# Prompt attention of a hybrid decoder layer: rounded high and low score operands, values as stationary half columns, output projection after the attention

## The chip, the cores and the metric

One core of one Trainium2 chip. The metric is the device time of one execution in microseconds (us). Before the change the kernel took 1881.82, 1887.27 and 1888.38 us in three runs, so the median is 1887.27 us. The profile is of another execution of the same program, which took 1884.58 us.

## The reference

One layer in float32 over a prompt of 1024 tokens and 8 sample sequences of one token each, width 1024. What matters here, shortened:

```python
z = rmsnorm(x, norm1_g) @ w_in                      # u, v, q, three pairs of k and v, gates
o_a = gmlp_mix(u, v, ...)                           # 512 columns
s = einsum('bqgrd,bngd->bgrqn', q, k_c) * scale     # 8 heads of 64, 2 key groups
p_c = masked_softmax(s - slopes * dist, dist >= 0)  # compressed branch, 63 keys
imp = einsum('bgqn,nj->bgqj', sum(p_c, axis=2), overlap)
_, idx = lax.top_k(imp, 8)                          # selected branch: 8 of 16 blocks of 64
o_s = softmax over the selected blocks @ v_s
o_w = softmax over the last 512 keys @ v_w          # window branch
o_b = gate0 * o_c + gate1 * o_s + gate2 * o_w
x = x + concat(rmsnorm(o_a), rmsnorm(o_b)) @ w_out
h = rmsnorm(x, norm2_g)
y = rmsnorm(x + (silu(h @ w_gate) * (h @ w_up)) @ w_down, final_norm_g)   # inner width 2816
```

The sample sequences go through the same weights, with keys from a paged cache. The new rows of keys and values are outputs too.

## The kernel before, in words

The five engines have one program each, written out by hand and tied by semaphores. There are five stages, and each engine goes through them in order.

**Stage 1** (lines 298 to 690) normalizes nine row tiles (eight of 128 prompt rows, one of the 8 sample rows), turns them, and multiplies them with w_in in five column chunks (`project`, line 324; the matmul is line 338). A matmul's stationary operand is the turned rows, so the sample tile has 8 stationary columns and still streams all columns of the chunk. `turn_k` (L351) turns the keys into `kT`: 64 rows of key, and 33 rows from a constant that carry position and block (`kaug`), 97 in all. At the end POOL loads a first part of the compressed cache (`load_raw`, L752), behind the store at L555.

**Stage 2** (L719 to 898) builds compressed keys and values; its last group is the prompt. **Stage 3** (L998 to 1259) is the samples' attention. There PE multiplies four sequences in four 32-column strips of its array, with `tile_position` (L1121, L1124, L1129).

**Stage 4** is the prompt's attention in eight query blocks i of 128 rows. One list `events` fixes the order on every engine. A block has 17 units: window heads 0 to 7 (up to 5 key tiles), the compressed branch, selected heads 0 to 7 (i+1 key tiles). For a head, in this order:
- `QK` (L1421): scores of one head, 128 queries by up to 1024 keys, a plain float32 matmul with 97 rows contracted; mask tiles are added by a bf16 matmul (L1426). It writes one of two bank pairs, which it shares with `QT`, `CS`, `SELT`, `OBT`, `WO` and `H2T`.
- DVE takes the row maximum (L1669), ACT the exponential and the row sum (L1552), into one of two buffers.
- `T` (L1490; L1488 for the compressed branch): PE turns each 128 by 128 piece of the probabilities; DVE (L1533) and ACT (L1537) copy the turned pieces out.
- `PV` (L1511, L1507): the turned probabilities are stationary (128 columns), the values of one head stream (64 columns): one matmul for each head and key tile.

At a branch's end `add_branch` (L1634 to L1645) scales and adds. Between the heads stand fillers: `QT` (L1398, copy L1657) turns the queries of the next block, `CS`, `CN`, `CI` (L1404 to L1408, L1595 to L1621) are the compressed softmax and the choice of blocks, `SELT` (L1432, L1676) brings that choice into the query rows. Also between the heads of block i stands the whole tail of tile i-1: `OBQ`, `OBN`, `OBT` (norm and turn of the result, L1443), `WO` (output projection, 16 float32 matmuls of 512 columns, L1452, added by L1696), `H2N` (L1701) and `H2T` (turn, L1470, split into high and low parts by L1573 and L1707).

**Stage 5** is the feed-forward part in 22 steps of 128 inner columns. All operands are split into a rounded high part (type fp32r) and a low part, and each product is three fp32r matmuls: gate and up at L1793 to L1795 (344 columns each), down at L1820 to L1822 (512 columns each). Down runs over nine row tiles and two halves, 18 units a step, each added to `x_all` by DVE (L1923). At the end each tile is normalized (L1934) and stored (L1773).

## Time and profile before

| what | value |
|---|---|
| profiled execution, device time | 1884.58 us |
| its span, first to last instruction | 1882.6 us |
| median of the runs | 1887.27 us |
| PE busy | 1776.3 us, 94% |
| DVE, ACT, POOL busy | 728.5, 390.3, 273.5 us |
| mean granted clock of PE | 0.96 |
| stage 4, first query turn to first gate matmul | 538 to 1083 us |

PE is TensorE's matmul side and PEld its weight loads. Busy time of a group is the time that the union of its records covers; records of PE overlap, since each lasts until its results are out. So how often a matmul can start is read from start times in the timeline, or from a long run of one form. A plain float32 matmul has two records, a transpose and an fp32r matmul have one.

### The profile page before, as it was taken

What the parts mean: (1) busy time and instruction counts of PE and PEld (TensorE: products, weight loads), DVE (VectorE), ACT (ScalarE), POOL (GpSimd) and SP (SyncE); (2) the same over time, 40 slices, a digit from 0 to 9 for tenths busy, and PEclk for the clock granted to TensorE, in tenths of its full rate; (3) what the DMA queues carried; (4) which work ended last, traced back from release to release, by engine and by line L of the source; (5) the groups of instructions that cost most, each with busy time, mean ns of one, the idle gap of its engine ahead of it and who ended that gap; (6) DMA issues with size and microseconds to landing.
All of it is one profiled execution on the core that took longest, in us unless ns stands there. A gap on an engine that the chain in (4) does not pass through costs nothing.

```text
span 1882.6 us, 25099 instructions
## 1 busy us (share of the span) xinstructions
PE 1776.3 (94%) x9317; PEld 1356.1 (72%) x9317; DVE 728.5 (39%) x1319; ACT 390.3 (21%) x862; POOL 273.5 (15%) x286
## 2 busy tenths in 40 slices
PE   7999999698778899999999899999999999999996
PEld 4464454587346666687776698998998998998894
DVE  2100334222224444574565215335335334334437
ACT  2100111122112323332332222112112112112112
POOL 2210121211300000000000113113113112112112
PEclk9999999698967999999999999999999999999999
DMA  8220100533630000000000121211211211211202
GB/s 294 78 89 0 45 1 6 141 90 109 188 107 4 4 4 1 4 4 1 4 1 1 34 68 34 68 33 33 67 33 33 67 33 33 67 33 33 67 11 90
DMA packets 91320, 94.73 MB, mean 50 GB/s; under 512 B 6353, under 2 KB 74546, under 8 KB 91154
## 3 DMA queue, kind: packets, MB, share of 16 engines
q1 hardware_dynamic: 69410, 73.99, 12.8%
q0 software_dynamic: 4240, 11.32, 2.0%
q10 hardware_dynamic: 17600, 8.47, 1.7%
q8 instruction: 46, 0.75, 0.2%
q14 instruction: 24, 0.19, 0.0%
HBM read 86.61 MB, written 11.34 MB: 52 GB/s over the span
## 4 chain that ended last, share of the span: by engine, by line
PE 86%; DVE 5%; issue 3%; DMA 2%; ACT 1%; SPq 1%; ACTq 1%; POOL 0%; POOLq 0%; DVEq 0%
PE bankpair L338 14%; PE bankpair L1793 9%; PE bankpair L1795 9%; PE bankpair L1794 9%; PE bankpair L1452 7%; PE bankpair L1421 6%; PE bankpair L1820 5%; PE bankpair L1511 5%; PE bankpair L1821 5%; PE bankpair L1822 5%; PE bankpair L819 3%; PE bankpair L1490 2%; DMA work<-in_state_win_kv 1%; PE bankpair L1408 1%; PE bankpair L803 1%
## 5 line engine op out<-in xcount | busy, mean ns | idle before, releaser
L1793 PE MATMUL bankpair<-h2T_high,w_high 128*128 128x344 f32 x1056 | 337.9, 320 | 0.0
L1795 PE MATMUL bankpair<-h2T_high,w_low 128*128 128x344 f32 x1056 | 337.1, 319 | 0.0
L1794 PE MATMUL bankpair<-h2T_low,w_high 128*128 128x344 f32 x1056 | 337.1, 319 | 0.0
L338 PE MATMUL bankpair<-work 128*128 128x512 f32 (+3 forms) x720 | 288.2, 557 | 0.8 <-DMA work<-in_w_in 0.8
L1923 DVE TENSOR_TENSOR x_all<-x_all,bankpair 128x512 f32<-128x512 f32 (+1 forms) x396 | 251.7, 684 | 1.7
L338 PEld LDWEIGHTS bankpair<-work 128*128 128x128 f32 (+1 forms) x720 | 127.2, 180 | 145.5 <-issue 136.6
L1909 DVE TENSOR_TENSOR kT_space<-kT_space,bankpair 128x344 f32<-128x344 f32 x66 | 33.9, 513 | 451.4 <-ACT kT_space L1857 451.4
L1793 PEld LDWEIGHTS bankpair<-h2T_high,w_high 128*128 128x128 f32 x1056 | 198.6, 188 | 3.1 <-issue 0.2
L1794 PEld LDWEIGHTS bankpair<-h2T_low,w_high 128*128 128x128 f32 x1056 | 198.1, 188 | 1.1 <-issue 0.2
L1795 PEld LDWEIGHTS bankpair<-h2T_high,w_low 128*128 128x128 f32 x1056 | 198.4, 188 | 0.0
L1844 POOL TENSOR_TENSOR w_low<-work,w_high 128x1024 fp32r<-128x1024 f32 x44 | 105.5, 2421 | 565.5 <-ACT w_high L1839 565.5
L1820 PE MATMUL bankpair<-w_high,act_high 128*128 128x512 f32 (+1 forms) x396 | 158.6, 401 | 3.5 <-DVE x_all L1923 3.5
L1421 PE MATMUL bankpair<-kT_space,work 97*128 97x512 f32 (+3 forms) x384 | 152.6, 503 | 9.8 <-ACT work L1552 3.7
L1857 ACT ACTIVATE kT_space<-bankpair 128x344 f32<-128x344 f32 x66 | 30.3, 459 | 624.3 <-PE bankpair L1795 624.3
L1821 PE MATMUL bankpair<-w_low,act_high 128*128 128x512 f32 (+1 forms) x396 | 157.3, 397 | 0.0
L1822 PE MATMUL bankpair<-w_high,act_low 128*128 128x512 f32 (+1 forms) x396 | 156.0, 394 | 0.0
L1552 ACT ACTIVATE work<-bankpair,small 128x640 f32<-128x640 f32 (+7 forms) x128 | 89.4, 699 | 188.4 <-DVE small L1669 183.4
L1669 DVE TENSOR_REDUCE small<-bankpair 128x1 f32<-128x640 f32 (+7 forms) x128 | 89.9, 704 | 67.4 <-PE bankpair L1426 67.0
L205 POOL TENSOR_SCALAR small<-small 128x1 f32<-128x1 f32 (+1 forms) x45 | 12.6, 280 | 610.1 <-ACT work L1562 371.9
L1421 PEld LDWEIGHTS bankpair<-kT_space,work 97*128 97x128 f32 x384 | 64.9, 202 | 45.0 <-issue 33.3
L1820 PEld LDWEIGHTS bankpair<-w_high,act_high 128*128 128x128 f32 (+1 forms) x396 | 70.0, 177 | 33.8 <-DVE x_all L1923 14.7
L1822 PEld LDWEIGHTS bankpair<-w_high,act_low 128*128 128x128 f32 (+1 forms) x396 | 70.1, 177 | 21.7
(270 smaller groups left out, 2064.3 us busy)
## 6 DMA issues: line engine op xcount, KB each, us to landing
work<-in_w_gate SPq DMA_DIRECT2D x22, 512.0 KB, 5.0
work<-in_w_up SPq DMA_DIRECT2D x22, 512.0 KB, 6.2
work<-in_w_down SPq DMA_DIRECT2D x22, 512.0 KB, 3.8
work<-in_w_in SPq DMA_DIRECT2D x4, 2048.0 KB, 7.9
x_all<-in_x_prompt SPq DMA_DIRECT2D x8, 512.0 KB, 12.2
work<-in_cache_kv_cmp SPq DMA_DIRECT2D x32, 128.0 KB, 2.8
work<-in_cache_kv_cmp POOLq DMA_DIRECT2D x32, 128.0 KB, 2.9
work<-in_cache_kv_slc POOLq DMA_DIRECT2D x32, 128.0 KB, 3.7
```

Of the source, the lines that this page charges most:

```text
L338: ins = pe.matmul(pb(at_n % 4)[0:n, 0:w], hT[:, k, P * t:P * t + n], wslot[c % 2][:, k, 0:w], start=(k == 0), stop=(k == KD - 1))
L1421: ins = pe.matmul(s_pair(e)[:, P * c:P * (c + len(part))], q, kT[0:KAUG, 2 * (kind == "w") + g, P * part[0]:P * part[-1] + P], start=True, ...
L1452: ins = pe.matmul(s_pair(e)[0:n, 512 * half:512 * half + 512], lhs, wo[:, k, 512 * half:512 * half + 512], start=(k == 0), stop=(k == KD - 1))
L1511: ins = pe.matmul(bank_o[:, DH * h:DH * h + DH], pT_buf[n % 4][:, col:col + P], v_all[:, tiles[b], int(kind == "w"), DH * g:DH * g + DH], ...
L1793: pe.matmul(out, wh, high, start=(k == 0), stop=False)
L1794: pe.matmul(out, wh, low, start=False, stop=False)
L1795: ins = pe.matmul(out, wl, high, start=False, stop=(k == KD - 1))
L1820: pe.matmul(out, ah, wh, start=True, stop=False)
L1821: pe.matmul(out, ah, wl, start=False, stop=False)
L1822: pe.matmul(out, al, wh, start=False, stop=True).then_inc(y_ready, 1)
L1844: pool.tensor_tensor(w_low[s][x], w_raw[s][x], w_high[s][x].bitcast(F32), ALU.subtract).then_inc(gu_low, 1)
L1923: dve.tensor_tensor(x, x, bank[2 + (s + t) % 2][0:n, 512 * half:512 * half + 512], ALU.add).then_inc(y_added, 1)
```

## The change

- **Scores.** The queries are rounded (`qT_split`, the same rounded part in both halves of the partitions), and their remainder goes into `qT_aug` with the 33 position rows. The keys are split likewise: `kT_split` holds the rounded part in rows 0 to 63 and the remainder in rows 64 to 127, `kT_aug` the rounded part and the 33 rows. QK and CS become two fp32r matmuls each, with 128 and 97 rows. For this each key or query is turned twice by plain matmuls with the identity, one into each column half of the array.
- **Values.** `T` and `PV` go by key tile ("item") and no longer by head: `T` turns the pieces of 4 heads for each of two key groups; `PV` has the values of a group as stationary operand (64 columns, one column half for each group) and streams 4 heads' probabilities, 512 columns. So all heads' probabilities of a branch are kept (`p_win`, `p_slc`), and the items of one branch stand between the score heads of the next. The result comes out turned: ACT copies it (`OC`), PE turns it back (`ON`), then DVE scales and adds.
- **Output projection.** All `WO`, `H2N`, `H2T` come after the last attention block. `x_all` holds the split operands meanwhile, so the prompt's x is loaded again. The position rows of the queries are loaded by POOL's queue.
- **Sample rows.** In `project`, `WO` and down the 8 sample rows go through the array in four strips, each with a quarter of the columns; down for them is plain float32, one unit for each step in place of two. The sample tile comes first in the last additions.

```diff
@@ project
+                for b in range(NQ):
+                    rows_b, cols_b = strip(b), slice(w // NQ * b, w // NQ * (b + 1))
+                    ins = pe.matmul(pb(at_n % 4)[rows_b, 0:w // NQ], hT[:, k, SEQ:TOK], wslot[c % 2][:, k, cols_b],
+                                    start=(k == 0), stop=(k == KD - 1))
@@ turn_k
-                ins = pe.transpose(pb(6 + m % 2)[0:DH, P * g:P * g + P], kvst[:, m % 2, col + DH * g:col + DH * g + DH],
-                                   ident[:, :])
+                for b in range(2):
+                    ins = pe.matmul(pb(6 + m % 2)[DH * b:DH * b + DH, P * g:P * g + P],
+                                    kvst[:, m % 2, col + DH * g:col + DH * g + DH], ident[:, :], start=True, stop=True,
+                                    tile_position=(0, DH * b), skip_group_check=True)
@@ take_kT
+            link(dve.tensor_copy(split, src))
+            dve.tensor_copy(kT_aug[0:DH, 2 * c:2 * c + 2, P * t:P * t + P], split[0:DH])
+            dve.tensor_tensor(split[DH:P], src[DH:P], split[DH:P].bitcast(F32), ALU.subtract).then_inc(kT_ready, 1)
@@ the order of stage 4
+    def half(i, kind, done, between):
+        heads = [unit_at[i, kind, h] for h in range(NH)]
+        parts = [n for b in done for n in branch_items(b)]
+        for k in range(max(NH, len(parts))):
+            if k < NH:
+                events.append(("QK", heads[k]))
+            if k == 0 and heads[0] > 0:
+                events.append(("EX", heads[0] - 1))
+            events.extend(between.get(k, []))
+            if 0 < k <= len(parts):
+                events.append(("PV", parts[k - 1]))
+                events.extend(branch_end(parts[k - 1]))
+            if k < len(parts):
+                events.append(("T", parts[k]))
+            if k < NH - 1:
+                events.append(("EX", heads[k]))
...
+        half(i, "w", [(i - 1, "s")] if i else [], {7: [("SELT", i)] if i >= 4 else []})
+        between = {0: [("ON", last)] if i else [], 1: [("OBQ", tail), ("OBN", tail)], 2: [("QT", i + 1)], 3: [("OBT", tail)],
+                   6: [("CS", i + 1)], 7: [("CN", i + 1), ("CI", i + 1)]}
+        between.setdefault(nw + 1, []).append(("ON", branch_at[i, "w"]))
+        half(i, "s", [(i, "w"), (i, "c")], between)
+        events.append(("ON", branch_at[i, "c"]))
...
+    for n, t in enumerate(tail_tiles):
+        if n >= 2:
+            events.append(("WO", t))
+        if n >= 1:
+            events += [("H2N", tail_tiles[n - 1]), ("H2T", tail_tiles[n - 1])]
@@ QK
+                    pe.matmul(out, qT_split[:, i % 2, g, cols], kT_split[:, 2 * (kind == "w") + g, keys],
+                              start=True, stop=False, skip_group_check=True)
+                    ins = pe.matmul(out, qT_aug[0:KAUG, i % 2, g, cols], kT_aug[0:KAUG, 2 * (kind == "w") + g, keys],
+                                    start=False, stop=not masks, skip_group_check=True)
@@ T and PV
+        for g in range(NG):
+            if n >= 1:
+                pe.wait_ge(pt_taken[g], n)
+            for r in range(NR):
+                    ins = pe.transpose(pb(4 + g)[:, cols], probs(kind)[:, h, P * b:P * b + P], ident[:, :])
+            ins.then_inc(pt_ready[g], 1)
...
+            pe.wait_ge(pt_taken[g], n + 1)
+            ins = pe.matmul(out[DH * g:DH * g + DH, :], v, p, start=(b == 0), stop=last, tile_position=(0, DH * g),
+                            skip_group_check=True)
@@ stage 4, SP and POOL
+        sp.wait_ge(s_ready, s_at["QK", len(units) - 1] + 1)
+        for t in range(NT):
+            sp.dma_start(x_all[:, t, :], x_dram(t)).then_inc(x_in[t], 16)
+        load_qaug(pool, 0)
+        load_qaug(pool, 1)
@@ down, sample unit
+            for b in range(NQ):
+                ins = pe.matmul(y_part(s, 0)[strip(b), 0:DQ], act_raw[s][:, SEQ:TOK], w_raw[s][2][:, 0, DQ * b:DQ * b + DQ],
+                                start=True, stop=True)
+            ins.then_inc(y_ready, 1)
```

## Rows read from the trace of the kernel before

**Rows 1.** The page: engines' busy time, granted clock of PE over the span.

```profile
PE 1776.3 (94%) x9317; PEld 1356.1 (72%) x9317; DVE 728.5 (39%) x1319; ACT 390.3 (21%) x862; POOL 273.5 (15%) x286
PEclk9999999698967999999999999999999999999999
```

**Rows 2.** Busy time by window: length, PE, PEld, DVE, ACT, POOL, PEclk, DMA.

```profile
14.00:338.00 324.00, 314.97 (x979) 156.59 (x977) 79.55 (x134) 53.24 (x101) 53.19 (x91) 0.99 0.19 65
456.00:538.00 82.00, 56.89 (x464) 34.40 (x464) 22.87 (x64) 11.21 (x20) 18.01 (x25) 0.81 0.50 142
538.00:1083.00 545.00, 517.87 (x2915) 365.93 (x2916) 268.38 (x477) 159.86 (x412) 17.56 (x36) 0.94 0.04 14
1092.00:1870.00 778.00, 773.67 (x4309) 698.33 (x4307) 320.17 (x534) 128.89 (x212) 158.27 (x78) 1.00 0.15 44
...
570.00:605.00 35.00, 30.81 (x154) 24.78 (x152) 17.49 (x43) 9.88 (x38) 0.72 (x2) 0.66 0.02 4
762.00:834.00 72.00, 71.00 (x447) 52.76 (x447) 44.08 (x84) 22.91 (x59) 1.48 (x4) 1.00 0.01 5
```

**Rows 3.** Timeline of block 7, one head with 1024 keys: start, duration.

```profile
1045.63 1.94 PE L1421 MATMUL bankpair<-kT_space,work 97*128 97x512 f32 x4
1047.41 0.22 PE L1426 MATMUL bankpair<-mask_diag,ident_bf 128*128 128x128 bf16 x1
1047.47 1.04 PE L1490 MATMUL bankpair<-ident,work 128*128 128x128 f32 x8
1047.66 1.23 DVE L1669 TENSOR_REDUCE small<-bankpair 128x1 f32<-128x1024 f32 x1 [2.62 <-PE bankpair L1426]
1048.35 1.90 PE L1511 MATMUL bankpair<-v_all,samp 128*128 128x64 f32 x16
1048.81 0.68 DVE L1533 COPY work<-bankpair 128x512 f32<-128x512 f32 x1
1048.92 1.11 ACT L1552 ACTIVATE work<-bankpair,small 128x1024 f32<-128x1024 f32 x1 [2.75 <-DVE small L1669]
1050.08 1.94 PE L1421 MATMUL bankpair<-kT_space,work 97*128 97x512 f32 x4
```

**Rows 4.** Groups of PE by form, whole span: count, busy us, mean ns.

```profile
L1511 PE MATMUL bankpair<-v_all,samp 128*128 128x64 f32 x528 | 69.2, 276 | 4.7 <-ACT samp L1537 3.8 <-DVE samp L1533 0.9
L338 PE MATMUL bankpair<-work 128*8 128x512 f32 x64 | 28.1, 592 | 0.0
L338 PE MATMUL bankpair<-work 128*8 128x280 f32 x16 | 3.9, 399 | 0.0
```

**Rows 5.** Timeline of stage 5, fp32r matmuls in a row.

```profile
1140.54 0.39 PE L1821 MATMUL bankpair<-w_low,act_high 128*128 128x512 f32 x1
...
1140.77 0.39 PE L1822 MATMUL bankpair<-w_high,act_low 128*128 128x512 f32 x1
```

**Rows 6.** Timeline of stage 3, four column strips, clock 1.00 here.

```profile
532.83 2.81 PE L1129 MATMUL bankpair<-work 128*8 128x128 f32 x96
```

**Rows 7.** Groups of DVE by form, 538 to 1083 us.

```profile
L1669 DVE TENSOR_REDUCE small<-bankpair 128x1 f32<-128x640 f32 x40 | 32.9, 822 | 21.5 <-PE bankpair L1426 21.2
L1701 DVE SCALAR_TENSOR_TENSOR work<-x_all,small,norm_g 128x1024 f32<-128x1024 f32 x7 | 9.0, 1279 | 1.2 <-POOL small L207 1.2
L1696 DVE TENSOR_TENSOR x_all<-x_all,bankpair 128x1024 f32<-128x1024 f32 x7 | 8.5, 1221 | 101.7 <-PE bankpair L1452 101.7
```

**Rows 8.** Timeline, the end of stage 4.

```profile
1062.01 0.69 DVE L1641 TENSOR_TENSOR work<-bankpair,small 128x512 f32<-128x512 f32 x1 [3.02 <-PE bankpair L1511]
...
1083.04 0.72 PE L1793 MATMUL bankpair<-h2T_high,w_high 128*128 128x344 f32 x1
```

**Rows 9.** Timeline, the end of stage 1.

```profile
324.49 7.03 PE L338 MATMUL bankpair<-work 128*8 128x512 f32 x16
...
333.40 0.59 POOL L555 DMA_DIRECT2D out_s_gmlp_v<-work  x1 [2.43 <-DVE work L651]
...
336.12 0.63 POOL L752 DMA_DIRECT2D work<-in_cache_kv_cmp  x1 [1.23 <-issue]
```

More of the change, by code:

```diff
@@ L828, in compressed @@
                 pe.wait_ge(vc_ready, w)
[L829 to L830 removed]
+            for b in range(1 if w < NW - 1 else 2):
+                pe.matmul(pb(6)[DH * b:DH * b + DH, 0:m * CMP_N].rearrange("p (m n) -> p m n", m=m), w2[0],
+                          hid[0][:, 0:m, 0:CMP_N], start=True, stop=True, tile_position=(0, DH * b))
             for j in range(m):
@@ L1300, in build_program, with branch_end @@
+    def branch_end(n):
+        b = items[n][:2]
+        if n != branch_items(b)[-1]:
+            return []
+        return [("OC", branch_at[b])]
     for i in range(NT):
+        half(i, "w", [(i - 1, "s")] if i else [], {7: [("SELT", i)] if i >= 4 else []})
+        last = branch_at[i - 1, "s"] if i else None
+        nw = len(key_tiles(i, "w"))
         tail = NT if i == 0 else i - 1
-        for place, name in ((3, "OBQ"), (4, "OBN"), (5, "OBT"), (6, "WO"), (8, "H2N"), (10, "H2T")):
-            before.setdefault(NU * i + place, []).append((name, tail))
@@ L1320, in build_program @@
-    events += [(name, NT - 1) for name in ("OBQ", "OBN", "OBT", "SPLIT", "WO", "H2N")]
-    events += [("GU", 0), ("H2T", NT - 1), ("GU", 1)]
-    s_at, p_at, pt_at, o_at = {}, {}, {}, {}
-    n_pt = 0
+        between = {0: [("ON", last)] if i else [], 1: [("OBQ", tail), ("OBN", tail)], 2: [("QT", i + 1)], 3: [("OBT", tail)],
+                   6: [("CS", i + 1)], 7: [("CN", i + 1), ("CI", i + 1)]}
+        if i + 1 == NT:
+            between = {k: v for k, v in between.items() if k < 6 and k != 2}
@@ new lines, in build_program, with exp_in_time @@
+    events += [("H2N", NT - 1), ("GU", 0), ("H2T", NT - 1), ("GU", 1)]
+    s_events = ("QT", "CS", "QK", "SELT", "ON", "OBT", "WO", "H2T")
+    def exp_in_time(planned):
+        out, pairs = [], []
+        for e in planned:
+            if e[0] == "EX" and e in out:
+                continue
+            if e[0] in s_events:
+                if len(pairs) >= 2 and pairs[-2][0] == "QK" and ("EX", pairs[-2][1]) not in out:
+                    out.append(("EX", pairs[-2][1]))
+                pairs.append(e)
+            out.append(e)
+        return out
@@ L1326, in build_program @@
+    events = exp_in_time(events)
+    s_at, p_at = {}, {}
     for e in events:
-        if e[0] in ("QT", "CS", "QK", "SELT", "OBT", "WO", "H2T"):
+        if e[0] in s_events:
             s_at[e] = len(s_at)
@@ new lines, in add_tile, with add @@
+        def add_tile(j, s, t, first):
+            for half in range(2):
+                u = y_unit(t, half)
+                x = x_all[:, t, 512 * half:512 * half + 512]
+                dve.wait_ge(y_ready, j * YH + (u + 1))
+                if not first:
+                    dve.wait_ge(y_added, j * YH + (u + 1 - YH))
+                dve.tensor_tensor(x, x, y_part(s, u), ALU.add).then_inc(y_added, 1)
+        def add(j, s, first=False):
+            add_samples(j, s, first)
+            for t in range(NT):
+                add_tile(j, s, t, first)
```

505 lines of the change are left out of this document (280 added, 225 removed).

## The prediction

> **What bounds the kernel now.** The page first: PE is busy for 1776 of 1883 us, DVE for 728, and the granted clock is 9 or more tenths in most slices, with dips around slices 8 to 16 [rows 1]. The windows by stage say where PE still has room: stage 1 is 315 of 324 us, stage 3 only 57 of 82, stage 4 518 of 545, stage 5 774 of 778 [rows 2]. So stages 1, 4 and 5 are bound by PE, and any PE time removed there comes off until the next engine is met. In stage 4 DVE has 268 and ACT 160 us of 545; these don't bind now, but they will be nearer. The timeline of one late head shows how dense PE is there: scores at 1045.63, turns at 1047.47, values at 1048.35, the next head at 1050.08 [rows 3], 4.45 us without a gap.
>
> **Prices of PE, from start times.** A float32 matmul of 512 columns: a head's two run from 1045.63 to the mask's start at 1047.41, and less a first 0.06 that is 0.86 us each [rows 3]. An fp32r matmul of 512 columns starts 0.23 us after the last [rows 5]. Eight transposes take 0.88 us until the next group starts, 0.11 each; sixteen records of values take 1.73, so 0.22 for one matmul of 64 streamed columns: these are held by the weight loads, not by the columns [rows 3]. The whole span agrees: 528 such records are busy for 69 us [rows 4]. Four strips side by side: 96 records of 128 columns in 2.81 us, 0.029 each, where one alone needs 0.11 [rows 6]. That is 3.7 times, so strips do run together, in plain float32 too.
>
> **Stage 1.** The 8-row matmuls are busy for 28.1 + 3.9 = 32.0 us [rows 4]. As 160 strip matmuls of two records: 320 x 0.029 = 9.3. That is 22.7 less. The last chunk's 5 us I don't count: POOL's load for stage 2 (336.12) stands behind its store of the sample rows (333.40), which waits for DVE, not for the last projection at 324.49 [rows 9]. Left: -17. The keys' turns grow from 32 transposes (3.5 us) to 64 float32 matmuls of two records; in pairs 64 x 0.11 = 7.0: +3.5, and +10.5 if pairs don't overlap. Two more DVE copies a tile lie in DVE's 75% of idle time [rows 2]. ACT's four small copies in place of one are spread over four banks. Sum -13.5. Three more DVE steps at the end of stage 2 lie on the way into stage 3: +1.
>
> **Stage 4, the attention.** Before, 545 us hold nine `WO` and `H2T` less the last turn. A `WO` is 16 x 0.86 = 13.8, with its turns 14.7; eight of them lie among the heads (118), the ninth in the tail from 1062.0 to 1083.0 [rows 8]. So the attention itself takes 524 - 118 = 406 us, and the tail 21.
>
> After it, two kinds of slots. With an item (66 beside a head, 8 at the end): `T` 8 x 0.11 = 0.87, `PV` 2 x 0.43 = 0.86 with both column halves together, and before `PV` the copy of the turned piece, 0.68, which starts about 0.19 after the last turn is through (the record of the turns outlasts its slot by 0.16, and the row maximum starts 0.03 after the mask's record ends), and 0.13, my value, back to PE: 1.0 in all [rows 3]. The next head's scores lie in that gap: for 640 keys 0.46 + 0.23 + masks 0.1 = 0.8, for 1024 keys 0.92 + 0.06 = 0.98. So a slot is 1.0 + 0.87 + 0.87 = 2.74 us, and 74 of them 203. It was 4.45 for a late head; but a late block has 13 items beside 16 heads. The 62 head slots without an item go through two banks: half of scores, row maximum, exponential and three handovers, for 640 keys (0.7 + 0.82 [rows 7] + 0.8 + 0.3)/2 with masks 1.4, for 1024 keys (0.98 + 1.23 + 1.11 + 0.3)/2 = 1.8 [rows 3], for one tile 0.65; summed over the blocks 63 us. Fillers: eight `QT` of 16 paired matmuls 1.75 plus 1.5 of waiting for ACT's and DVE's takes of 1024 columns = 26; `CS`, `CN`, `CI` 5 each block = 40, since DVE waits in its order for the exponential; 24 `ON` of 0.44 plus half a microsecond of lost bank = 21; `OBT` and `SELT` 13. Together 203 + 63 + 100 = 366. The early blocks have short heads, and there the clock is low already (0.66 from 570 to 605, PE busy 88%; 1.00 from 762 on [rows 2]); with `WO` gone from them I add 12. So 378 against 406: -28. PE's own work in it falls much more, from 358 to some 255 us by these prices; the rest is given back to waits.
>
> Covers: DVE's row maxima and copies are 1.5 to 1.9 us of a 2.74 us slot, ACT's exponential and copy 1.6 to 1.9. Without this cover nothing else hides them. The position rows on POOL's queue wait behind nothing that matters, POOL has 18 us of work in 545 [rows 2]. The reload of x (4 MB on SP) starts at the last scores, with 21 us of items and the sample `WO` ahead of its first reader: nothing.
>
> **The tail.** Now all `WO` stand here: 3.5 for the samples (8 groups of 4 strips, 0.43 each), 8 x 13.8 = 110, turns 8 x 0.87 = 7, entry with `ON` 2. And a new wait: `H2T` of tile t-1 needs `H2N`, which DVE's order puts behind the addition of `WO` t. So PE idles after each `WO` for 1.22 + 1.28 [rows 7] + 0.3 = 2.8 us, eight times, 22.5. Sum 145, where the tail was 21 and 118 lay in the blocks: 139, +6. Stage 4 in all -22.
>
> **Stage 5.** Each step loses six fp32r matmuls of 512 columns, 1.38 us, and gains four strips of 256 float32 columns, 0.43: -0.95 x 22 = -21. DVE loses an addition too, so it stays level with PE (three matmuls 0.69, an addition 0.69). The last store is of 128 rows and no longer of 8: +1.
>
> **Sum.** -13.5 + 1 - 22 - 21 + 1 = -54.5. Against the profiled execution's own 1884.6 (1882.6 of span and 2 around it) that is 1830. The median of the runs lies 2.7 higher, so I say 1833.
>
> **What I could not read.** Whether two halves of 64 columns overlap as four strips do: between 0.86 (together) and 1.72 (one after the other) an item; I take 0.86, by rows 6. What it costs to go from the whole array to halves and back, twice an item: nothing at the low end; at the high end a pipe that runs empty, the 0.16 by which a record of eight transposes (1.04) outlasts the 0.88 to the next start [rows 3], 148 x 0.16 = 24 us. I take nothing, for no row shows a stop there. The Trainium skill says in "TensorEngine Tiling (Array Packing)", Key Properties, that changing the tiling mode drains TensorE; no run here shows it with nothing else to wait for, and by it the time would go toward 1857.
>
> **Rivals.**
> - *Attention as dense as now.* The order keeps PE filled: work of 255 and the same 48 us of loss as before (406 less 358) give 303, 75 less than my 378: 1758. For it: PE hardly waits today [rows 2]. Against: DVE has more to do beside each filler. 0.12.
> - *The half columns don't overlap.* 74 x 0.86 = 64, `QT` +14, keys +7: 1918. Rows 6 speak against it. 0.04.
> - *The clock.* Slower than before: PE stands still for part of every slot, and the clock goes to its lower level of 1.2 GHz in the attention, as in stage 3, where PE is busy for 69% and the clock is 0.81 [rows 2]. An item slot then has 1.5 + 3.5 = 5.0 in place of 2.74, 74 slots +167 us. With half of them at the lower level +84: 1917. It decides from 33% of the slots on (54.5/167). For it: 0.66 at 570 us. Against: stage 3 has long stops, and these gaps are under 1 us. 0.09.
> - *Waits pile up.* The next scores can't start in the copy's gap, since their bank is late (ACT's copy goes ahead of the exponential in its order): 66 x 0.8 = 53 more: 1886, no change. For it: ACT and DVE are strictly in order with 1.9 of 2.74 us used. 0.08.
> - *The drain*, 24 us, and a few microseconds of each of these: 1857, still faster; part of my case.
>
> My case has 0.67, its own range 1778 to 1875. Within 0.5% of 1887 is about what a measurement can tell from no change, so faster means under 1878. Faster 0.67 + 0.12 = 0.79 less what of my case ends near no change, 0.03: 0.76. Same: the waits' 0.08 and some of that, 0.10. Slower 0.14: the clock and the halves, and 0.01 of the waits. The range for 8 in 10 reaches from 1762 to 1888.
>
> **What would show it.** Right: two fp32r records of 512 columns 0.23 apart in the scores; `PV`'s two groups starting within 0.05 of each other; item slots of 2.7 us in late blocks; gaps of 2.8 us before each `H2T`; a down phase with one short sample unit; stage 4 of about 523 us. Wrong: `PV` groups one behind the other; a granted clock under 0.85 over the attention; PE waiting on ACT's exponential in most slots; stage 4 at 545 or over, or under 470.

## The result and the profile after

The changed kernel takes 1913.55 us (median of 4 runs, 1909.34 to 1917.5) against 1884.9 us for the kernel before in the same session: a ratio of 1.0151 (1.0118 to 1.0184, the 95% interval, as for all ratios below). It is slower by 1.5%, where 1833 was forecast and the range ended at 1888. The two profiled executions differ by 24.9 us of span (1907.5 and 1882.6). In the rows PE is TensorE, DVE is VectorE, ACT is ScalarE and POOL is GpSimd.

The page after, engine totals and granted clock in 40 slices, answers to [rows 1]:

```profile
PE 1708.9 (90%) x9131; PEld 1273.0 (67%) x9131; DVE 720.8 (38%) x1313; ACT 420.7 (22%) x879; POOL 279.2 (15%) x296
PEclk9999998798868888978999999999999999999998
```

PE has 67 us less to do in the records, and the kernel is longer. The windows by stage (length; busy time of PE, PEld, DVE, ACT, POOL; PEclk) say where, as [rows 2] did: stage 1, stages 2 and 3, the attention up to its last values matmul, the tail up to the first gate matmul, stage 5.

```profile
0.00:342.00 342.00, 306.68 (x1344) 166.59 (x1345) 97.33 (x176) 62.51 (x131) 60.88 (x113) 0.96 0.26 83
342.00:528.70 186.70, 153.48 (x1033) 118.96 (x1031) 47.88 (x163) 37.99 (x117) 36.73 (x58) 0.89 0.38 112
528.70:974.50 445.80, 357.89 (x1956) 229.72 (x1956) 231.85 (x410) 168.19 (x385) 9.32 (x22) 0.83 0.06 21
974.50:1124.60 150.10, 128.37 (x395) 59.20 (x393) 32.86 (x39) 19.93 (x30) 12.45 (x22) 0.97 0.06 19
1124.60:1892.90 768.30, 762.10 (x4411) 698.55 (x4409) 304.36 (x519) 129.31 (x212) 157.61 (x76) 1.00 0.16 46
```

Against the forecast, in us: stage 4 starts 9.5 earlier (12.5 forecast); the attention takes 445.7 (378); the tail 150.1 (145); stage 5 is 17.5 shorter (21); the end +0.8 (+1). The misses are 3.0 + 67.7 + 5.1 + 3.5 - 0.2 = 79.1, and the attention has 67.7 of them. PE is busy there for only 80% at a granted clock of 0.83, where before it was 0.94 over the stage. The start of stage 4 scatters from trace to trace (526.4 to 534.2 us among the kernels below that have the same first three stages), so the first of these terms is known to some 4 us; the last projection matmul of stage 1 ends at 307.2, before at 315.3.

The waits of PE in the attention (instruction, releaser: us in total, times, longest):

```profile
PE bankpair L1535 <- ACT work L1661: 52.6, 53, 3.0
PE bankpair L1556 <- ACT work L1661: 13.7, 9, 3.4
```

L1535 is the first score matmul of a head, L1556 the turning back of a branch's output (`ON`), L1661 the exponential. Both wait for a bank pair that a head's exponential has yet to read. The timeline of block 6 shows the longest of them:

```profile
880.33 0.28 PE L1521 MATMUL bankpair<-kcT_aug,qT_aug 97*128 97x64 f32 x1
881.57 0.69 DVE L1718 TENSOR_TENSOR work<-bankpair,small 128x512 f32<-128x512 f32 x1
882.30 0.63 ACT L1651 ACTIVATE work<-work 128x512 f32<-128x512 f32 x1 [3.85 <-DVE work L1718]
882.83 0.99 ACT L1661 ACTIVATE work<-bankpair,small 128x896 f32<-128x896 f32 x1
883.97 1.11 PE L1556 MATMUL bankpair<-ident,work 128*128 128x128 f32 x4 [3.37 <-ACT work L1661]
885.01 1.97 PE L1628 MATMUL bankpair<-samp,vc_p 63*64 63x512 f32 x4
```

ACT's written order has the exponential of the compressed scores (L1651) ahead of the head's (L1661), and the first waits for three steps of DVE. PE stands for 3.37 us, up to 883.97, and at 883.1 the clock falls. Granted clock, two windows of the same kernel:

```profile
883.10:900.20 17.10, 13.88 (x43) 7.83 (x44) 9.76 (x23) 3.99 (x8) 0.00 (x0) 0.50 0.00 0
900.30:915.00 14.70, 14.70 (x95) 8.93 (x94) 7.58 (x10) 6.87 (x15) 0.00 (x0) 1.00 0.01 1
```

0.50 is the lower level, 1.2 GHz, for 17.1 us from the end of the stop on; then 2.4 GHz again. There are 13 such stretches in the attention, 153.6 us in all; before there were 54.6 us.

An item's slot at the full clock, block 6:

```profile
901.83 1.08 PE L1628 MATMUL bankpair<-samp,v_all 128*64 128x512 f32 x4
902.84 1.09 PE L1612 MATMUL bankpair<-ident,work 128*128 128x128 f32 x8
903.53 0.60 ACT L1642 ACTIVATE work<-bankpair 128x512 f32<-128x512 f32 x1 [1.50 <-PE bankpair L1612]
903.69 0.48 PE L1535 MATMUL bankpair<-kT_split,qT_split 128*128 128x512 f32 x1
```

Values 1.01, turns 0.85, and 1.01 from the scores to the next values, so 2.87, where 2.74 was forecast. The halves do overlap (the second record of a pair starts 0.06 after the first), but an item takes 1.01 and not 0.86.

### The profile page after: what moved, and what is told of

It is laid out like the page before. It is cut to its first block, busy times and chain, and to the rows that moved or that the text cites. A ratio compares the mean times of both kernels' runs of the same rounds, so it can differ in the third digit from the quotient of the medians.

```text
span 1907.5 us, 24568 instructions
## 1 busy us (share of the span) xinstructions
PE 1708.9 (90%) x9131; PEld 1273.0 (67%) x9131; DVE 720.8 (38%) x1313; ACT 420.7 (22%) x879; POOL 279.2 (15%) x296
## 4 chain that ended last, share of the span: by engine, by line
PE 83%; DVE 6%; issue 4%; ACT 4%; DMA 2%; ACTq 1%; POOL 0%; POOLq 0%; SPq 0%; DVEq 0%
PE bankpair L356 13%; PE bankpair L1923 9%; PE bankpair L1925 9%; PE bankpair L1924 9%; PE bankpair L1574 6%; PE bankpair L1628 5%; PE bankpair L1964 4%; PE bankpair L1966 4%; PE bankpair L1965 4%; PE bankpair L1612 3%; PE bankpair L868 3%; ACT work L1661 3%; PE bankpair L1535 2%; PE bankpair L1537 2%; DMA work<-in_state_win_kv 1%
## 5 line engine op out<-in xcount | busy, mean ns | idle before, releaser
L356 PE MATMUL bankpair<-work 128*128 128x512 f32 (+1 forms) x640 | 257.7, 559 | 0.6 <-DMA work<-in_w_in 0.6
L2075 DVE TENSOR_TENSOR x_all<-x_all,bankpair 128x512 f32<-128x512 f32 x352 | 224.7, 682 | 1.2
L356 PEld LDWEIGHTS bankpair<-work 128*128 128x128 f32 x640 | 120.4, 191 | 123.5 <-issue 116.8
L1964 PE MATMUL bankpair<-w_high,act_high 128*128 128x512 f32 x352 | 141.6, 402 | 5.3 <-DVE x_all L2075 5.3
L1535 PE MATMUL bankpair<-kT_split,qT_split 128*128 128x512 f32 (+3 forms) x192 | 88.9, 463 | 62.3 <-ACT work L1661 52.6
L1966 PE MATMUL bankpair<-w_high,act_low 128*128 128x512 f32 x352 | 139.1, 395 | 0.0
L1965 PE MATMUL bankpair<-w_low,act_high 128*128 128x512 f32 x352 | 138.6, 394 | 0.0
L1535 PEld LDWEIGHTS bankpair<-kT_split,qT_split 128*128 128x128 f32 x192 | 43.6, 227 | 93.0 <-ACT work L1661 75.5
L1612 PEld LDWEIGHTS bankpair<-ident,work 128*128 128x128 f32 x528 | 69.5, 163 | 48.6 <-issue 40.5
L1661 ACT ACTIVATE work<-bankpair,small 128x640 f32<-128x640 f32 (+7 forms) x128 | 89.1, 696 | 46.3 <-DVE small L1788 45.4
L1964 PEld LDWEIGHTS bankpair<-w_high,act_high 128*128 128x128 f32 x352 | 66.0, 188 | 32.8 <-issue 9.5
```

The source lines that it names most:

```text
L356: ins = pe.matmul(pb(at_n % 4)[:, 0:w], hT[:, k, P * t:P * t + P], wslot[c % 2][:, k, 0:w], start=(k == 0), stop=(k == KD - 1))
L1535: pe.matmul(out, qT_split[:, i % 2, g, cols], kT_split[:, 2 * (kind == "w") + g, keys], start=True, stop=False, skip_group_check=True)
L1612: ins = pe.transpose(pb(4 + g)[:, cols], probs(kind)[:, h, P * b:P * b + P], ident[:, :])
L1661: taken(act.activation(probs(kind)[:, h, 0:w], s_pair(("QK", a))[:, 0:w], ACT.Exp, bias=neg_max[:, n % 4:n % 4 + 1], accum_out=row_sum(i, ...
L1964: pe.matmul(out, ah, wh, start=True, stop=False)
L1965: pe.matmul(out, ah, wl, start=False, stop=False)
```

## How the attention's time is split up

For each form of PE instruction I take the time to the next start (or to its own end, where PE then stood) in stretches at the full clock, and multiply the mean by the count. That is PE's **work**. What PE is busy beyond it is the loss by the **clock**; the rest is **idle**. Together they are the attention. It is an accounting of one profiled execution each, from its records, and I trust it to about 5 us. A matmul that a wait follows counts up to its own end, so work depends a little on where the waits lie.

The labels are those of the experiments below: before_wo_last is the kernel before with the late projection alone, heads_again the changed kernel with the values by head again, and the others are the changed kernel with one edit or, from three on, several (stops is heads_again with forced stops).

| kernel | work | clock | idle | attention | at the lower clock | tail | median |
|---|---|---|---|---|---|---|---|
| before_wo_last | 358 | 15 | 16 | 389.6 | 38 | 141.4 | 1877 |
| heads_again | 324 | 28 | 23 | 374.7 | 65 | 129.7 | 1827 |
| changed kernel | 303 | 55 | 88 | 445.7 | 154 | 150.1 | 1914 |
| plain_scores | 346 | 53 | 78 | 476.6 | 133 | 146.8 | 1941 |
| act_order | 303 | 44 | 72 | 418.6 | 113 | 150.0 | 1886 |
| on_own | 308 | 40 | 78 | 426.0 | 116 | 150.1 | 1887 |
| pad_on | 324 | 47 | 81 | 451.8 | 126 | 151.2 | 1920 |
| one_score | 280 | 60 | 97 | 436.2 | 181 | 150.1 | 1905 |
| tail_order | 304 | 52 | 88 | 444.0 | 150 | 131.5 | 1898 |
| three | 308 | 38 | 64 | 411.2 | 92 | 132.7 | 1856 |
| exp_first | 300 | 45 | 63 | 408.1 | 126 | 132.7 | 1855 |
| spread | 308 | 35 | 62 | 404.6 | 85 | 129.7 | 1849 |
| stops | 324 | 62 | 31 | 417.5 | 143 | 129.7 | 1869 |

## The experiments

**The projection last, alone** (before_wo_last). The kernel before, with `WO`, `H2N` and `H2T` taken from the blocks and put after the attention, the `H2N` ahead of the next `WO`'s addition:

```diff
-        for place, name in ((3, "OBQ"), (4, "OBN"), (5, "OBT"), (6, "WO"), (8, "H2N"), (10, "H2T")):
+        for place, name in ((3, "OBQ"), (4, "OBN"), (5, "OBT")):
```

> The kernel before, with WO, H2N and H2T of all tiles after the last attention block (turned results kept in q_all, the norm's step put ahead of the next addition in DVE's order). Nothing else of the change is in it. Theory P (the projection between the heads was what kept PE dense and its clock up): blocks 0 to 3 then stall and run at the lower clock, attention and tail together 25 us or more longer than before's 545 us, total 1910 or more. Rival (heads of the old form keep PE busy by themselves, 4.45 us a late head without a gap): within 10 us of the kernel before, 1878 to 1895, lower clock in the attention no more than 70 us.

Measured: 1877.32 us, ratio 0.9965 (0.9941 to 0.999), 0.7 us under the rival's range, with 38 us at the low clock, so the rival holds. The attention falls from 523.4 to 389.6 and the tail grows from 21.4 to 141.4. The heads keep PE filled without the projection between them, so it covered nothing, and moving it is not what cost. The prediction took 406 us for the attention without the projection; it is 389.6, so the eight `WO` with their turns had added 134 us among the heads and not 118. That error cancels in its sum, where the same 118 leaves the attention and is counted with the tail.

**ScalarE's order** (act_order). The changed kernel, the head's exponential ahead of that of the compressed scores:

```diff
+                if e[0] == "CS" and pairs and pairs[-1][0] == "QK" and ("EX", pairs[-1][1]) not in out:
+                    out.append(("EX", pairs[-1][1]))
                 pairs.append(e)
```

> The changed kernel with one step moved on ACT alone: the exponential of head 6 ahead of that of the compressed scores, so that the bank which ON of the window branch needs is free 3 us sooner in each of seven blocks. Theory W (only waits count): at most 7 x 2.5 = 17 us less, 1896 or more. Theory C (each stop of about 3 us also brings the clock down to its lower level for 7 to 17 us after it): the attention has 153 us at the lower level now; this falls to under 90, and the time by 25 to 50 us, to 1865 to 1888.

Measured: 1885.64 us, ratio 1.0012 (0.9994 to 1.0031), 28 less than the changed kernel. The 13.7 us of waits of `ON` became 4.1 + 3.5:

```profile
PE bankpair L1537 <- ACT work L1663: 39.4, 47, 2.4
PE bankpair L1558 <- ACT work L1663: 4.1, 6, 1.5
PE bankpair L1558 <- DVE work L1720: 3.5, 4, 1.1
```

Idle fell by 16 and the loss by the clock by 11. The time is in theory C's range and 10 us under what theory W allows; C's low clock of under 90 us did not come true (113).

**Work in the place of the stop** (pad_on). Before the `ON` of the window branch, 24 transposes whose results nobody reads, so that PE works where it waited (some 21 us of work in 8 blocks):

```diff
+            if name == "ON" and branches[a][1] == "w":
+                pe.wait_ge(o_copied, a + 1)
+                for r in range(24):
+                    pe.transpose(...)
```

> The changed kernel with 24 transposes more on PE, of no use, ahead of ON's wait for its bank, in each block (into the bank that has just been copied out): 192 x 0.11 = 21 us of added work at the full clock, put where PE waits. Theory W: the work lies in waits of about 3 us in most blocks and costs 0 to 8 us, the time is 1913 to 1922. Theory C: with PE active in the stop the clock stays up, the lower level falls from 153 us to under 100, and the kernel gets faster by 10 to 35 us although PE does more, 1880 to 1904.

Measured: 1920.16 us, 1.0179 (1.0144 to 1.0214). The low clock fell from 154 to 126 us and idle by 7, but together they gave back 15 of the 21 added. The time is in theory W's range; theory C's, with a low clock of under 100 us, was missed. Filling a stop with useless transposes doesn't pay here; no other filling was tried.

**One rounded score matmul in place of two** (one_score). What is left out is the product of the rounded queries with both parts of the keys, that is the main part of the scores; it shows a time and no usable kernel:

```diff
-                    pe.matmul(out, qT_split[:, i % 2, g, cols], kT_split[:, 2 * (kind == "w") + g, keys],
-                              start=True, stop=False, skip_group_check=True)
...
-                                    start=False, stop=not masks, skip_group_check=True)
+                                    start=True, stop=not masks, skip_group_check=True)
```

> The changed kernel without the first of the two score matmuls of each head (the product of the rounded queries with the keys is left out of the scores of the window and selected branches): 192 fp32r matmuls fewer, about 88 x 0.23 + 24 x 0.17 + 80 x 0.11 = 33 us of PE at the full clock. If PE bounds the attention: 33 us less, or 45 with what lies at the lower clock, 1868 to 1880. Theory W (bank, row maximum and exponential set the pace): 15 us less or under, 1898 or more. Theory C beside it: PE is less active, so the lower clock grows over 153 us.

Measured: 1905.49 us, 1.0108 (1.0078 to 1.0137): 8 us for 23 of work. Idle grew by 9 and the loss by the clock by 5: 14 of the 23 come back. Theory W holds, and the low clock grew, to 181 us, as theory C had it: with less work for PE the waits and the clock take most of the gain.

**The tail's order** (tail_order). `H2N` of a tile ahead of the next `WO`'s addition in DVE's order:

```diff
+        if n >= 1:
+            events.append(("H2N", tail_tiles[n - 1]))
         if n >= 2:
             events.append(("WO", t))
         if n >= 1:
-            events += [("H2N", tail_tiles[n - 1]), ("H2T", tail_tiles[n - 1])]
+            events.append(("H2T", tail_tiles[n - 1]))
```

> The changed kernel with H2N of tile t-1 ahead of the addition of WO t in DVE's order (nothing else). The trace has 18.2 us of PE waiting for H2N in the tail, seven times 2.6 us. If these waits are what their row says, the tail falls from 150 to 134 us and the time by 14 to 18, to 1896 to 1900; PE then waits 0.5 us for its bank after each turn. If the clock is pulled down by these stops as well, 20 or more.

Measured: 1897.79 us, 1.0061 (1.004 to 1.0081), 16 less than the changed kernel and as expected. The waits of PE in the tail, first of the changed kernel, then of this one:

```profile
PE bankpair L1595 <- DVE work L1829: 21.0, 8, 2.8
```

```profile
PE bankpair L1597 <- DVE work L1831: 2.7, 1, 2.7
PE bankpair L1576 <- DVE x_all L1819: 2.6, 6, 0.4
```

The new wait was there as forecast, eight times, 21.0 against 22.5.

**`ON` in a bank of its own** (on_own), the branch's own output bank, off the pair of bank pairs that the scores go through:

```diff
-s_events = ("QT", "CS", "QK", "SELT", "ON", "OBT", "WO", "H2T")
+s_events = ("QT", "CS", "QK", "SELT", "OBT", "WO", "H2T")
...
-                    ins = pe.transpose(s_pair(e)[:, P * r:P * r + P], oT[:, P * r:P * r + P], ident[:, :])
+                    ins = pe.transpose(pb(6 + a % 2)[:, P * r:P * r + P], oT[:, P * r:P * r + P], ident[:, :])
```

> The changed kernel with ON (the turn back of a branch's result) written into the bank that it was copied from, no longer into one of the two bank pairs which the scores use; 24 turns less in that ring. Theory R (each filler in the ring of two bank pairs puts row maximum and exponential of a head onto PE's path): 24 x about 1.2 us of waits less, and with the clock 30 to 50 us, to 1863 to 1885, low clock under 110 us. Rival (DVE's and ACT's program order sets the waits, not the banks): under 12 us, 1902 or more.

Measured: 1887.25 us, 1.0013 (0.9998 to 1.0028), 26 less, 2 us outside theory R's range and 15 from its rival's; the low clock is 116 us, where R had under 110. The waits of `ON` for an exponential are gone. New ones of values matmuls for DVE's copy (L1639) take 14 us of it back:

```profile
PE bankpair L1536 <- ACT work L1662: 46.1, 43, 3.0
PE bankpair L1629 <- DVE work L1639: 7.1, 2, 3.7
PE bankpair L1629 <- DVE samp L1639: 6.7, 3, 3.1
```

**All three edits** (three: ScalarE's order, the tail's order, `ON` in its own bank):

> The three edits together: ACT's order at the compressed scores (-28 alone), H2N ahead of the addition in the tail (14 to 18), ON in its own bank (30 to 50 by theory R, under 12 by its rival; the first edit frees the same bank in seven of 24 cases, so not all adds). By theory R 1835 to 1855, faster than the kernel before; by the rival 1860 to 1872.

Measured: 1856.07 us, 0.9844 (0.9819 to 0.987), between the two ranges, 1 us from theory R's. Singly they gave 28 + 16 + 26 = 70, together 57; the first and the third both shorten the wait in front of `ON`. The design of the change can beat the kernel before, with two orders and one bank changed.

**Only the values part undone** (heads_again). The changed kernel with turns and values of each head two and three slots late, as before, and the reordered tail; rounded scores, strips and the late projection stay:

```diff
-    items = [(i, kind, n) for i, kind in branches for n in range(1 if kind == "c" else len(key_tiles(i, kind)))]
...
+    for u in range(len(units) + 3):
+        events += before.get(u, [])
+        if u < len(units) and units[u][1] != "c":
+            events.append(("QK", u))
+        if 0 <= u - 2 < len(units):
+            events.append(("T", u - 2))
+        if 0 <= u - 3 < len(units):
+            events.append(("PV", u - 3))
...
-            ins = pe.matmul(out[DH * g:DH * g + DH, :], v, p, ..., tile_position=(0, DH * g))
+            ins = pe.matmul(bank_o[:, DH * h:DH * h + DH], pT_buf[n % 4][:, col:col + P], v_all[...], ...)
```

> The changed kernel with only its values part undone: probabilities are turned and multiplied head by head two and three slots late, as in the kernel before, with the reordered tail; the rounded scores, the sample strips and the late projection stay. Attention (start of stage 4 to the last values matmul) was 389.6 us with this form and plain scores, 445.7 in the changed kernel. One of the two rounded score matmuls was worth 33 us of PE work, so a plain one of four passes is worth some 120 and the split saves about 55. Theory V (the values part, its chain from exponential to turn and the clock that falls in its stops, is what costs): attention 330 to 355 us, low clock under 70 us, time 1790 to 1825. Rival S (the cheaper scores take the cover away in any form, so that the heads wait and the clock falls here too): attention 370 us or more, low clock over 100 us, time 1835 or more.

Measured: 1827.27 us (1818.77 to 1838.46, 4 runs), 0.971 (0.9659 to 0.9761). Of theory V the low clock (65) came true, but the attention is 374.7 and not 330 to 355: the two rounded matmuls took 34 us off PE's work and not 55. The rival's 370 us came true without its low clock of over 100. The time lies just above V's range. Against the tail_order kernel, which differs from this one in the values part alone, the attention is 69 us shorter and the time 71. The values part here is two things at once, the half columns and the order of turns, values and fillers that goes with them; this run undoes both. The profiled execution took 1819.21 us, 8 under the median. Its windows, attention and tail:

```profile
530.10:904.80 374.70, 352.20 (x2751) 313.27 (x2752) 237.18 (x440) 149.94 (x392) 9.32 (x22) 0.91 0.07 23
904.80:1034.50 129.70, 124.31 (x392) 58.08 (x391) 32.23 (x39) 17.50 (x27) 11.70 (x20) 0.99 0.07 24
```

**Only the scores undone** (plain_scores). The changed kernel with a plain float32 matmul on unrounded operands:

```diff
-                    pe.matmul(out, qT_split[:, i % 2, g, cols], kT_split[:, ...], start=True, stop=False, ...)
-                    ins = pe.matmul(out, qT_aug[0:KAUG, ...], kT_aug[0:KAUG, ...], start=False, ...)
+                    ins = pe.matmul(out, qT_aug[0:KAUG, ...].bitcast(F32), kT_aug[0:KAUG, ...].bitcast(F32), start=True, ...)
```

> The changed kernel with only its scores undone: one plain fp32 matmul per head and chunk on unrounded queries and keys, some 55 us more work of PE in the head slots; the values in half columns and everything else stay. Theory V (the head slots of this form end with the exponential's chain, not with PE's work): much of the added work fills waits, idle goes from 89 to 50 or less, low clock from 154 to 110 or less, attention 440 to 470 us, time 1908 to 1938. Rival S (PE's work sets the slot): attention 495 us or more, time 1960 or more.

Measured: 1941.01 us, 1.0305 (1.0279 to 1.0332); attention 476.6. It falls between the theories, 3 us above V's range and 19 under the rival's; V's idle time of 50 and low clock of 110 did not come true (78 and 133). Work rose by 43, idle fell by 10 and the clock's loss by 2: a quarter of the added work filled waits. So of the 43 us that the split takes off PE, 31 reach the time in this form, and in the form by heads 15 of 34 (from before_wo_last, 389.6 to 374.7), where the clock took back 13 and idle 6. Since the profile of heads_again is of a short execution, these 15 may be some 9 in a typical one.

**Exponential first** (exp_first). On the three edits, in an item's slot the head's exponential ahead of ACT's copy of the turned piece:

```diff
-            if k < len(parts):
-                events.append(("T", parts[k]))
             if k < NH - 1:
                 events.append(("EX", heads[k]))
+            if k < len(parts):
+                events.append(("T", parts[k]))
```

> The kernel with the three edits (attention 411 us, 65 us of idle on PE, 92 us at the low clock, 1856 us), and in every slot of an item ScalarE takes the head's exponential ahead of its copy of the item's turned probabilities. Theory A (the order of ScalarE's work in a slot sets when the score bank comes free): the 28 us that score matmuls waited for the exponential fall by half or more, attention 385 to 403 us, time 1830 to 1848. Rival B (it is the length of the chain and the lack of work of PE in slots without an item; and the copy taken later makes the values matmul wait instead): attention 406 to 420 us, time 1850 to 1866.

Measured: 1854.53 us, 0.9831 (0.9814 to 0.9847), the same as the three edits; idle 63 and 64. Rival B holds, by its second part. The waits of PE, first with the three edits, then with this one too (L1540 is the first score matmul, L1633 the values, L1666 the exponential, L1643 and L1647 the two copies of the turned piece):

```profile
PE bankpair L1540 <- ACT work L1666: 28.4, 35, 2.4
PE bankpair L1633 <- DVE samp L1643: 7.9, 4, 3.6
PE bankpair L1633 <- DVE work L1643: 7.7, 3, 3.8
```

```profile
PE bankpair L1633 <- ACT samp L1647: 18.9, 9, 5.8
PE bankpair L1540 <- ACT work L1666: 15.5, 27, 2.4
PE bankpair L1633 <- ACT work L1647: 12.6, 6, 5.7
```

The order of the two does set when the scores can start: their waits fall from 28.4 to 15.5 us. But the values now wait 31.5 us for ScalarE's copy, where they waited 15.6 for DVE's, and nothing is gained.

**Items spread over the head slots** (spread), on the three edits, where a half block has fewer than 8 of them:

```diff
+        if kind == "w" and 0 < len(parts) < NH:
+            slots = {NH * j // len(parts): j for j in range(len(parts))}
...
+            if k in slots:
+                events.append(("T", parts[slots[k]]))
```

> The kernel with the three edits, and in the half of a block whose heads score the window, where fewer than 8 items of the last block lie (blocks 1 to 7), the items stand spread over the 8 head slots instead of in the first ones. Theory A (slots that hold a head alone are bound by its chain of maximum and exponential, and an item laid there fills it): 7 halves with 4 slots without an item on average are not fewer, but the waits of two such slots in a row go; attention 398 to 408 us, time 1843 to 1853. Rival B (the number of slots without an item is what counts, and it is the same): attention 409 to 415 us, time 1853 to 1860.

Measured: 1848.86 us, 0.9807 (0.9791 to 0.9824), 7 less than the three edits; attention 404.6 and the time both as theory A had them. Idle fell by 2 and the clock's loss by 3, so how spreading gains isn't clear from the trace beyond these.

**A stop by itself** (stops). heads_again, in which PE waits once a block for a chain of five one-column powers on GpSimd:

```diff
+            if name == "STOP":                      # on PE, ahead of the scores of selected head 4
+                pe.wait_ge(stopped, a + 1)
+            if name == "STOP":                      # on GpSimd
+                pool.wait_ge(s_ready, stop_at[e] + 1)
+                for r in range(5):
+                    ins = pool.tensor_tensor(idle, idle, minus_half[:, 0:1], ALU.pow)
...
+                ins.then_inc(stopped, 1)
```

> The kernel with the old values part (heads_again: attention 374.7 us, 65 us at the low clock, 23 us of idle, 1827 us), in which PE is made to wait once in each of the 8 blocks: after the scores of head 4 of the selected branch GpSimd runs a chain of five one-column powers (0.56 us each, so some 3 us), and PE goes on when it is done. Nothing else is changed. Theory C (a stop of some 3 us brings the low clock after it, as in the changed kernel, where 13 stretches made 154 us of it): low clock over 110 us, attention longer than by the stops themselves (24 us less what other waits give back) by another 15 us or more, time 1860 to 1895. Rival W (a stop costs its own length and no more): low clock 60 to 85 us, attention longer by 16 to 26 us, time 1842 to 1855.

Measured: 1869.01 us (1861.27 to 1875.08, 7 runs), 0.9909 (0.9881 to 0.9937): 42 us more than heads_again. The waits, the window of the attention, and the start of one slot behind a stop:

```profile
PE bankpair L1501 <- POOL small L1676: 16.2, 8, 3.1
```

```profile
529.40:946.90 417.50, 386.13 (x2751) 345.85 (x2752) 238.97 (x440) 150.16 (x392) 33.39 (x62) 0.83 0.06 21
```

```profile
750.99 0.80 PE L1501 MATMUL bankpair<-kT_split,qT_split 128*128 128x512 f32 x1 [2.11 <-POOL small L1676]
...
759.25 0.77 PE L1501 MATMUL bankpair<-kT_split,qT_split 128*128 128x512 f32 x1
...
763.76 0.77 PE L1501 MATMUL bankpair<-kT_split,qT_split 128*128 128x512 f32 x1
```

The chain starts with the end of the scores of head 3, so turns and values cover a part of it: eight stops of 0.6 to 3.1 us, 2.0 in the mean and 16.2 together. The attention is 42.8 longer: idle +9, clock +34, PE's work the same. The low clock went from 65 to 143 us. The slot of selected head 5 in block 4, from 759.25 to 763.76, takes 4.51 us; the same slot in heads_again, at the full clock, 2.39:

```profile
732.09 0.48 PE L1491 MATMUL bankpair<-kT_split,qT_split 128*128 128x512 f32 x1
...
734.47 0.48 PE L1491 MATMUL bankpair<-kT_split,qT_split 128*128 128x512 f32 x1
```

So a stop of 2 us cost 5.3. Theory C holds. The clock's loss grew by 34 us for 79 more at the lower level, 0.43 of it. The Trainium skill puts that penalty at half of the time at the lower clock ("TensorE: Matmul & The Clock Gate", Terms); by that it would be 39. The clock did not fall behind the eighth stop, of 0.6 us.

## Why the prediction was wrong

**The attention, 378 forecast, 445.7 measured, is the step that failed**, in two of its terms. "PE's own work in it falls much more, from 358 to some 255": the 358 is right (358), but after the change it is 303, +48. "With `WO` gone from them I add 12" for the clock: the loss is 55, +43. What was "given back to waits", 111, was 88, -23. The sum is +68.

**PE's work.** The trace of after places the missing 48. Values are 296 records of 0.278 us, 82 us, where the case has 64 (74 items of 0.86): +18. The step between whole array and halves, taken as nothing, lies in these 0.15 to 0.25 an item; it isn't shown by itself, since no run has the same matmuls without the switch. The score matmuls are 80 us, where two rounded ones at the case's prices are 66: +14, of which 8 are the first one of each pair behind other work, 0.32 to the next start and not 0.23, 88 times; in heads_again, where no change of tiling mode is near them, they take 0.32 too. The 160 mask records count 0.145 and not 0.07, since what follows them is now a gap (0.07 in heads_again): +12. The turns take 0.117 and not 0.11: +4. So in the form by items PE's work is only 21 less than by heads (303 and 324): the values take 82 us for 128, but the masks take 12 more and `ON`, which the form by heads hasn't, another 12.

**The clock.** The rival named it, with a chance of 0.09 and the argument "these gaps are under 1 us". In the changed kernel 34 gaps are over 1 us (59 us of the 88 idle), where before there were 4 (6 us); most of the idle time waits for the exponential, as at 883.97. The rival's point of decision was a third of the slots at the lower clock, 54.5 us; 154 of 446 us is 34%, and the loss is 43 more than the case had. So its mechanism came true, and most of its size. The clock alone would have brought 1833 to 1876; with PE's work it passes 1885. The stops run shows the mechanism by itself, in the form by heads. Three of the prediction's own signs of being wrong stand in the trace: the clock of 0.83, 53 waits of scores for the exponential, and a stage 4 of 595.9 us.

**The waits.** "Waits pile up" named ACT's strict order and a bank that comes late. The bank does come late: the scores wait 52.6 us for it. But to change the order that the rival named, the copy ahead of the exponential, brought nothing (exp_first); another one did, the exponential of the compressed scores ahead of the head's, in front of `ON`, worth 28 us by the act_order run. The case had its waits as idle time, and too much of it rather than too little. It priced each at its length, with nothing for what the clock does behind it, and that was the error of reading.

**What held.** The projection's move costs no cover (before_wo_last). The tail: 150.1 for 145, and the wait of 2.8 eight times is 21.0 of 22.5; that it was worth 16 us to avoid by one line is seen only by trying. The strips of stage 1: 8.6 + 1.2 us of records, where 9.3 was forecast [rows 4]:

```profile
L361 PE MATMUL bankpair<-work 128*8 128x128 f32 x256 | 8.6, 292 | 0.0
L361 PE MATMUL bankpair<-work 128*8 128x70 f32 x64 | 1.2, 224 | 0.0
```

The score matmuls 0.23 apart, and the halves side by side: both right, and not enough. Stage 5 saved 0.93 a step, where 0.95 was forecast. From one step's first gate matmul to the next it is some 35.46 us before and 34.49 to 34.56 after:

```profile
1142.39 0.32 PE L1793 MATMUL bankpair<-h2T_high,w_high 128*128 128x344 f32 x1
...
1177.85 0.32 PE L1793 MATMUL bankpair<-h2T_high,w_high 128*128 128x344 f32 x1
```

```profile
1182.76 0.32 PE L1923 MATMUL bankpair<-h2T_high,w_high 128*128 128x344 f32 x1
...
1217.26 0.32 PE L1923 MATMUL bankpair<-h2T_high,w_high 128*128 128x344 f32 x1
```

What is missing of the 21 lies in the last step, where PE waits 6.2 us for additions and not 3.5. The sample unit in the timeline of stage 5:

```profile
1170.69 0.32 PE L1925 MATMUL bankpair<-h2T_high,w_low 128*128 128x344 f32 x1
1170.94 0.62 PE L1952 MATMUL bankpair<-work,kT_space 128*8 128x256 f32 x8
1171.49 0.50 PE L1964 MATMUL bankpair<-w_high,act_high 128*128 128x512 f32 x1
1171.83 0.39 PE L1965 MATMUL bankpair<-w_low,act_high 128*128 128x512 f32 x1
```

The unit is 0.55 and not 0.43; 0.25 before it stand for 0.157, and 0.34 behind it for 0.23. Other units of down got shorter by a little, which makes up for it; why isn't traced. The Trainium skill's rule that a change of tiling mode drains TensorE ("TensorEngine Tiling (Array Packing)", Key Properties) fits the 0.25 and the 0.15 to 0.25 an item: 11 to 18 us for 74 items, under the 24 of the case's high end. It isn't shown by them, and the 0.34 speaks little for it: an fp32r matmul behind float32 ones takes 0.32 in heads_again with no change of mode near.

**Which part of the change cost what.** In the attention, by the two-by-two of before_wo_last (389.6), heads_again (374.7), plain_scores (476.6) and the changed kernel (445.7): rounded scores save 15 or 31; the values part costs 71 or 87. More than half of that goes with order and banks, not with the half columns as such: with the same half columns the attention falls from 444.0 (tail_order) to 411.2 (three) and 404.6 (spread), where heads_again has 374.7. What the half columns would cost in the best order was not measured. Outside it the strips save 17.5 in stage 5 and most of the 9.5 in stage 1, and the late projection takes attention and tail from 544.8 to 531.0 with the better tail order, which is worth 19; with the change's own it would be some 5 worse than before. So the rounded scores, the strips and, with that order, the late projection pay. heads_again is these three, and at 0.971 it is the fastest kernel here.

## What to carry to other kernels

Price a stop of PE not by its length but by what the granted clock does behind it: in this kernel a stop of 2 us cost 5.3. When an edit takes work off PE in a stage where it is dense, list the gaps over 1 us that open up, each with its releaser, before counting the gain; here it was mostly a bank that ScalarE, in its fixed order, released late, and one exponential moved ahead on ScalarE gave back 28 us, as much as the whole change had lost. And test the parts of a large change one by one: here three good parts were hidden by one that cost more, and over half of its cost came back with other orders and one other bank.

## What the hardware showed unasked

- The clock stayed at the lower level for 17 us behind the stop of 3.4 us at 883, and for 3 to 27 us behind seven of the forced stops, of 1.1 to 3.1 us. In heads_again it did not fall once between 620 us and the end of the attention, though PE waited for 1.1 us at 641.6 and at 659.5; in stops it fell behind a stop of 1.1 us at 869.4. So the length of a stop alone doesn't decide.
- The loss by the clock is not half of every microsecond at the lower level: 4.51 against 2.39 us for a dense slot (47% of its time), but 55 of 154 us (36%) in the changed kernel, where some of that time is waiting anyway.
- Two float32 matmuls of 64 columns each in the two column halves start as pairs and take 1.01 us for four records of 512 columns, against 0.86 for one such matmul alone; side by side, but not free. The four strips of stage 1 take 9.8 us for 320 records, 0.03 each, as in [rows 6].
- heads_again's four runs lie between 1818.8 and 1838.5, 1.1% apart, where 19 of the kernel before in one session lay within 0.8%. The mean clock was 0.960 in the two shorter ones and 0.947 and 0.945 in the others, so the spread goes with the clock.
